# A hybrid DeltaNet and convolution layer: its 640 tokens go through the dense products as 128 and 512 columns in place of 320 and 320

## What is computed

```python
def _swiglu(h, w_in, w_out):
    a, b = jnp.split(h @ w_in, 2, axis=-1)
    return (jax.nn.silu(a) * b) @ w_out
...
    h = _rmsnorm(x, norm_ffn1) * (1 + sc1) + sh1
    x = x + 0.5 * gt1 * _swiglu(h, w_ffn1_in, w_ffn1_out)
    h = _rmsnorm(x, norm_mix) * (1 + sc2) + sh2
    m, s_f, s_b = _mixer(h, w_mix_in, ...)
    x = x + gt2 * m
    h = _rmsnorm(x, norm_ffn2) * (1 + sc3) + sh3
    x = x + 0.5 * gt3 * _swiglu(h, w_ffn2_in, w_ffn2_out)
```

## Time and profile before

| What | Value |
|---|---|
| Median of 2 runs | 1538.11 us (1537.68 to 1538.53) |
| Span of the profiled execution | 1540.2 us |
| TensorE matmuls, busy | 1444.7 us, 94% |
| TensorE weight loads, busy | 1395.0 us, 91% |
| VectorE, ScalarE, GpSimd busy | 41%, 25%, 10% |
| Matmul instructions | 9932 |

### The profile page before, as it was taken

The page is one execution under the profiler, slowest core; times in us unless marked ns, Lnnn a source line. Parts: engine busy times, 40 slices in busy tenths (PEclk is TensorE's granted clock), DMA queues, the critical chain, the costliest instruction groups (busy, mean ns, idle before and its releaser), DMA issues.

```text
span 1540.2 us, 23972 instructions
## 1 busy us (share of the span) xinstructions
PE 1444.7 (94%) x9932; PEld 1395.0 (91%) x9932; DVE 626.4 (41%) x995; ACT 385.1 (25%) x570; POOL 150.5 (10%) x113
## 2 busy tenths in 40 slices
PE   5699999999999969999997999987999999999996
PEld 3587899999999968999986999986999999999996
DVE  2722232333222255465585665446323332332222
ACT  3311211212111134453321212223222121212222
POOL 0300000000000030001334644003000000000000
PEclk9899999999999979999998999997999999999998
DMA  9488622222322211222545332121222222232211
GB/s 341 184 318 278 180 69 79 71 71 84 94 75 75 67 41 55 69 70 83 167 121 148 85 86 82 35 62 42 68 82 68 82 68 82 68 94 76 76 57 69
DMA packets 221201, 154.70 MB, mean 100 GB/s; under 512 B 22181, under 2 KB 207950, under 8 KB 217038
## 3 DMA queue, kind: packets, MB, share of 16 engines
q1 hardware_dynamic: 219680, 153.06, 32.4%
q10 hardware_dynamic: 1454, 0.68, 0.1%
HBM read 140.47 MB, written 13.24 MB: 100 GB/s over the span
## 4 chain that ended last, share of the span: by engine, by line
PE 87%; DVE 6%; ACT 2%; issue 2%; POOL 1%; DMA 1%; SPq 1%; ACTq 0%; DVEq 0%; POOLq 0%
PE ps L519 70%; PE ps L594 2%; PE ps L561 2%; PE ps L751 2%; PE ps L763 1%; PE ps L762 1%; DVE hf L1309 1%; DVE sub_tmp L1499 1%; PE ps L864 1%; PE ps L798 1%; DVE sub_x L1502 1%; POOL Tm L1790 1%; PE ps L800 1%; POOL NTa L1799 1%; PE ps L657 1%
## 5 line engine op out<-in xcount | busy, mean ns | idle before, releaser
L519 PE MATMUL ps<-h_hi,w_hi 128*128 128x320 f32 x1856 | 431.7, 314 | 9.6 <-DVE w_lo L1247 7.0
L519 PE MATMUL ps<-h_lo,w_hi 128*128 128x320 f32 x1856 | 424.7, 310 | 0.0
L519 PE MATMUL ps<-h_hi,w_lo 128*128 128x320 f32 x1856 | 424.3, 310 | 0.0
L1247 DVE TENSOR_TENSOR w_lo<-w_raw,w_hi 128x1024 fp32r<-128x1024 f32 (+1 forms) x156 | 207.8, 1333 | 430.7 <-ACT w_hi L919 429.4
L519 PEld LDWEIGHTS ps<-h_hi,w_hi 128*128 128x128 f32 x1856 | 311.6, 189 | 24.6 <-issue 18.8
L519 PEld LDWEIGHTS ps<-h_hi,w_lo 128*128 128x128 f32 x1856 | 312.1, 189 | 0.0
L519 PEld LDWEIGHTS ps<-h_lo,w_hi 128*128 128x128 f32 x1856 | 312.1, 189 | 0.0
L919 ACT ACTIVATE w_hi<-w_raw 128x1024 fp32r<-128x1024 f32 (+1 forms) x156 | 175.1, 1124 | 542.6 <-PE ps L519 474.8
L519 PE MATMUL ps<-g_hi,w_hi 128*128 128x320 f32 x704 | 160.9, 310 | 0.0
L519 PE MATMUL ps<-g_lo,w_hi 128*128 128x320 f32 x704 | 160.4, 309 | 0.0
L519 PE MATMUL ps<-g_hi,w_lo 128*128 128x320 f32 x704 | 160.3, 309 | 0.0
(11 more groups left out here) (221 smaller groups left out, 1271.2 us busy)
## 6 DMA issues: line engine op xcount, KB each, us to landing
w_raw<-in_w_ffn_in SPq DMA_DIRECT2D x88, 512.0 KB, 3.8
ada_w<-in_w_ada SPq DMA_DIRECT2D x32, 1024.0 KB, 6.9
w_raw<-in_w_ffn_out SPq DMA_DIRECT2D x32, 704.0 KB, 4.5
w_raw<-in_w_mix_in SPq DMA_DIRECT2D x28, 512.0 KB, 3.9
ada_w<-in_w_ada SPq DMA_DIRECT2D x8, 512.0 KB, 3.9
w_raw<-in_w_mix_out SPq DMA_DIRECT2D x8, 512.0 KB, 5.1
d_lt<-LTp SPq DMA_DIRECT2D x10, 256.0 KB, 2.4
d_qk<-QKp SPq DMA_DIRECT2D x10, 256.0 KB, 2.5
```

The lines of the kernel that those rows point to most:

```text
L519: last = pe.matmul(acc[a_slot][b], w, m[:, k0 + k, b * TH:b * TH + TH], start=start and k == 0 and n == 0, stop=stop and k == kt - 1 and n ...
L1247: nc.vector.tensor_tensor(w_lo[:, slot, 0:kt * P], w_raw[:, slot, 0:kt * P], w_hi[:, slot, 0:kt * P].bitcast(F32), ALU.subtract).then_inc( ...
```

## The change

The b loops take `PART[b]`, tokens 0 to 127 and 128 to 639, in place of two halves of 320. The first bank of an accumulator then holds the 128 context tokens and the second the 512 latent ones. The residual needs two instructions in place of three, the taps four in place of six. Everything else keeps its place and its count.

```diff
-TH = T // 2
+PART = (slice(0, TP), slice(TP, T))
...
-        acc = [[ps[2 * s][:, 0:TH], ps[2 * s + 1][:, 0:TH]] for s in (0, 1, 3)]
-        sums = [ps[4][:, 0:TH], ps[5][:, 0:TH]]
+        acc = [[ps[2 * s][:, 0:TP], ps[2 * s + 1][:, 0:TS]] for s in (0, 1, 3)]
+        sums = [ps[4][:, 0:TP], ps[5][:, 0:TS]]
...
-        PIECES = ((0, 0, TP, 0, 0), (0, TP, TH, 1, TP), (1, 0, TH, 1, TH))
...
                         for b in range(2):
-                            last = pe.matmul(acc[a_slot][b], w, m[:, k0 + k, b * TH:b * TH + TH],
+                            last = pe.matmul(acc[a_slot][b], w, m[:, k0 + k, PART[b]],
                                              start=start and k == 0 and n == 0,
                                              stop=stop and k == kt - 1 and n == 2)
...
                 for b in range(2):
-                    last = nc.scalar.activation(sa[:, b * TH:b * TH + TH], acc[0][b], ACT.Silu)
+                    last = nc.scalar.activation(sa[:, PART[b]], acc[0][b], ACT.Silu)
...
-                for bnk, b0, b1, i, t0 in PIECES:
+                for b in range(2):
                     last = nc.vector.scalar_tensor_tensor(
-                        out=x[:, j, t0:t0 + b1 - b0], in0=acc[a_slot][bnk][:, b0:b1], scalar=gate[:, m, j, i:i + 1],
-                        in1=x[:, j, t0:t0 + b1 - b0], op0=ALU.mult, op1=ALU.add)
+                        out=x[:, j, PART[b]], in0=acc[a_slot][b], scalar=gate[:, m, j, b:b + 1],
+                        in1=x[:, j, PART[b]], op0=ALU.mult, op1=ALU.add)
...
                 for step, (bnk, b0, b1, t0, tap) in enumerate((
-                        (0, 0, TP - 1, 1, before), (0, TP, TH, TP + 1, before), (1, 0, TH - 1, TH + 1, before),
-                        (0, 1, TP, 0, after), (0, TP + 1, TH, TP, after), (1, 0, TH, TH - 1, after))):
+                        (0, 0, TP - 1, 1, before), (1, 0, TS - 1, TP + 1, before),
+                        (0, 1, TP, 0, after), (1, 1, TS, TP, after))):
```

More of the change, by code:

```diff
@@ L593, in first_pair @@
                             for b in range(2):
-                                last = pe.matmul(acc[s][b], w, m[:, k, b * TH:b * TH + TH],
+                                last = pe.matmul(acc[s][b], w, m[:, k, PART[b]],
                                                  start=k == 0 and n == 0, stop=k == KD - 1 and n == 2)
@@ L690, in _ @@
                     for b in range(2):
-                        last = pe.matmul(sums[b], ones_t, (sa, uu)[n % 2][:, b * TH:b * TH + TH], start=True, stop=True)
+                        last = pe.matmul(sums[b], ones_t, (sa, uu)[n % 2][:, PART[b]], start=True, stop=True)
                     last.then_inc(ssm, 1)
@@ L698, in _ @@
                             for b in range(2):
-                                last = pe.matmul(sums[b][0:2 * NAB, :], wab_2[:, k, :, :], m[:, k, b * TH:b * TH + TH],
+                                last = pe.matmul(sums[b][0:2 * NAB, :], wab_2[:, k, :, :], m[:, k, PART[b]],
                                                  start=k == 0 and i == 0, stop=k == KD - 1 and i == 1)
@@ L1056, in _ @@
                     for b in range(2):
-                        last = nc.scalar.activation(abt[:, b * TH:b * TH + TH], sums[b][0:2 * NAB, :], ACT.Copy)
+                        last = nc.scalar.activation(abt[:, PART[b]], sums[b][0:2 * NAB, :], ACT.Copy)
                     last.then_inc(ab_ev, 1)
@@ L1091, in _ @@
                     for b in range(2):
-                        last = nc.scalar.activation(ss[:, n - 3, b * TH:b * TH + TH], sums[b], ACT.Copy)
+                        last = nc.scalar.activation(ss[:, n - 3, PART[b]], sums[b], ACT.Copy)
                     last.then_inc(ss_rdy, 1)
@@ L1103, in _ @@
                     for b in range(2):
-                        last = nc.scalar.activation(cv[:, b * TH:b * TH + TH], acc[2 if n == 2 else n % 2][b],
+                        last = nc.scalar.activation(cv[:, PART[b]], acc[2 if n == 2 else n % 2][b],
                                                     ACT.Identity, scale=tap)
@@ L1116, in _ @@
                     for b in range(2):
-                        last = nc.scalar.activation(zs[:, n - 12, b * TH:b * TH + TH], acc[n % 2][b], ACT.Silu)
+                        last = nc.scalar.activation(zs[:, n - 12, PART[b]], acc[n % 2][b], ACT.Silu)
                     last.then_inc(z_rdy, 1)
@@ L1125, in _ @@
                     for b in range(2):
-                        last = nc.scalar.activation(cc[:, b * TH:b * TH + TH], acc[n % 2][b], ACT.Copy)
+                        last = nc.scalar.activation(cc[:, PART[b]], acc[n % 2][b], ACT.Copy)
                     last.then_inc(cc_rdy, 1)
@@ L1333, in gate_out @@
                 for b in range(2):
-                    last = nc.vector.tensor_tensor(sa[:, b * TH:b * TH + TH], sa[:, b * TH:b * TH + TH], acc[1][b],
+                    last = nc.vector.tensor_tensor(sa[:, PART[b]], sa[:, PART[b]], acc[1][b],
                                                    ALU.mult)
@@ L1406, in taps @@
                 for step, (bnk, b0, b1, t0, tap) in enumerate((
-                        (0, 0, TP - 1, 1, before), (0, TP, TH, TP + 1, before), (1, 0, TH - 1, TH + 1, before),
-                        (0, 1, TP, 0, after), (0, TP + 1, TH, TP, after), (1, 0, TH, TH - 1, after))):
+                        (0, 0, TP - 1, 1, before), (1, 0, TS - 1, TP + 1, before),
+                        (0, 1, TP, 0, after), (1, 1, TS, TP, after))):
                     ins = nc.vector.scalar_tensor_tensor(out=cv[:, t0:t0 + b1 - b0], in0=a[bnk][:, b0:b1], scalar=tap,
                                                          in1=cv[:, t0:t0 + b1 - b0], op0=ALU.mult, op1=ALU.add)
-                    if step in (2, 5):
+                    if step in (1, 3):
                         link(ins)
@@ L1538, in _ @@
                     for b in range(2):
-                        last = nc.vector.tensor_tensor(uu[:, b * TH:b * TH + TH], cc[:, b * TH:b * TH + TH],
+                        last = nc.vector.tensor_tensor(uu[:, PART[b]], cc[:, PART[b]],
                                                        acc[a_slot][b], ALU.mult)
@@ L1559, in _ @@
                     for b in range(2):
-                        last = nc.vector.tensor_tensor(yc[:, m, b * TH:b * TH + TH], cv[:, b * TH:b * TH + TH],
+                        last = nc.vector.tensor_tensor(yc[:, m, PART[b]], cv[:, PART[b]],
                                                        acc[a_slot][b], ALU.mult)
```

## The result

The changed kernel takes 1718.24 us (median of 2 runs, 1717.95 to 1718.54) against 1538.11: 1.1167 of the time before, 95% interval 1.1146 to 1.1188. The forecast was 1711 us, in a range of 1680 to 1775.

The account below looks back on a forecast made before the run. TensorE's matmul pace was taken to bound the kernel: 4032 pairs going from 293.4 to 338 ns add 180 us, less 6 hidden and 1 saved, so 1538 + 173 = 1711 us, range 1680 to 1775.

Parts of the forecast that it names:

- the wide slot: Time from a 512-column fp32r matmul to the next matmul on TensorE, taken as 227 ns.
- The narrow slot: Time a 128-column matmul holds TensorE until the next matmul's weights are loaded, taken as 111 ns.
- only one load runs ahead: On TensorE, one weight load can run under the matmul before it, never two; read from rows behind line 657.
- rival 1: Two loads fit under a 512-column matmul, so the pair stays at 294 ns: 1537 us, chance 0.07.
- the low end: 128-column matmul at the bare weight load, 107 ns; with 15 us hidden 1687 us, range set from 1680.
- the tail of 162: Fixed 162 ns by which a matmul's recorded duration was taken to exceed its slot.
- the nearest row: Pricing the 512-column fp32r matmul, absent from the trace, by the bf16 one: 389 less 162 gives 227 ns.
- the upper end: 512-column matmul at 235 ns, if the 13.4 ns over its columns were a tenth of the stream.
- I let 7 us vanish: Taken off the 180 us: 6 us beside other work, 1 us for fewer residual and tap instructions.
- 4.7 (4 and 0.7): Mixing stage: 4 us hidden beside triangular solves and transfers, at most 0.7 us where units alternate with w_hi, w_lo and cv.
- The second: Narrow fp32r matmul falls to plain fp32's rate, 222 ns, pair 449 ns: 2156 us, chance 0.10.
- The third: Narrow matmul 124 ns or wide one 235, both 359 a pair: up to 1796 us; far end's chance 0.03.

Follow-up runs that it names:

- the two mirror-image runs: Changed kernel with 32 of 128 weight columns loaded in 3096 of 4032 pairs: for the 512-column matmul 1576.36 us, for the 128-column matmul 1723.84 us.

## Why the prediction was right

It was right in its sign, its mechanism and its size, 7 us under the first measurement and 11 under the second. But two terms of the sum were off by more than that, in opposite directions (over 4032 pairs the wide slot by 26 us, the narrow one by 17). That the size came out so near is in part luck.

**The narrow slot is the load.** Shown by the two mirror-image runs (1576 and 1724 us), by the line of the gate product, which kept its pace with 32 weight columns, and by the bend between 224 and 320 columns. The argument from the earlier trace rows that only one load runs ahead held too: with two, rival 1, the pair would have stayed at 294 ns.

**The durations of both slots were mis-sized, and their sum hardly.** I took 111 + 227 = 338. With the line from the runs a wide slot is 512 x 0.4516 + 2.2 = 233.4 ns, so 340.1 leaves 106.7 for the narrow one: the bare load of 128 x 0.833 that I had named as the low end. A second reading agrees. The wide matmuls of the run with 320 and 512 columns, where no load is bare, are recorded with this:

```profile
L520 PE MATMUL ps<-h_lo,w_hi 128*128 128x512 f32 x928 | 367.7, 396 | 0.0
```

Less the tail of 162 that is 234 ns. The changed kernel's are recorded with 443, 47 more, and 107 less the narrow stream's 60 (128 x 0.4516 + 2.2) is 47. The forecast that this group would last 389 ns on average failed for both reasons: the stream is longer than the bf16 row made it, and a matmul's record includes its wait for weights. The step that failed is "the nearest row": I let the bf16 matmul of 512 columns stand for fp32r, against the fp32r row of 320 columns scaled up (235), which I had as the upper end. The narrow slot's 111 came from plain fp32 matmuls of line 706, and the 4 ns over the load were not there. In the pair the errors were -6 and +4. The price of a load is not exact either: 106.7 fits 128 columns here, but the runs with 192 and 224 columns leave 109 and 110 ns for the narrow slot, and the load of 96 columns left 86 in place of 80.

**What is hidden.** I let 7 us vanish. 4032 x 46.7 ns are 188.3 us. The median grew by 180.1, so 8 us of them did not come; between the two kernels timed again (1722.33 against 1537.09) it grew by 185.2, so 3 did not; between the two profiled spans by 176.5, so 12 did not. The last figure is the least certain, because the profiled execution of the kernel before was a long one: its span alone is 2.1 us over the median of the times, where the changed kernel's is 1.5 under its own. So 7 is not shown to be wrong. The chain in order of time gives the places. The marks before and after:

```profile
621.82 42.24 PE ps L519 x288
816.59 0.89 SPq L337
949.37 0.39 issue
987.49 44.03 PE ps L519 x288
1031.54 1.15 DVE x L1376 x3
1068.14 336.19 PE ps L519 x2280
1523.81 1.15 DVE x L1376 x3
```

```profile
645.49 16.47 PE ps L593 x78
915.79 0.89 SPq L336
1046.66 0.40 issue
1086.54 49.24 PE ps L518 x288
1135.81 1.02 DVE x L1375 x2
1172.83 389.50 PE ps L518 x2280
1700.49 1.02 DVE x L1375 x2
```

| Stage, from mark to mark | Pairs | Due at 46.7 ns | Came |
|---|---|---|---|
| Inputs and first units, to 199.84 / 217.02 | 384 | 17.9 | 17.2 |
| The stretch of 2400 | 1200 | 56.0 | 56.0 |
| Residual, norm, first pair, to 585.21 / 661.96 | 48 | 2.2 | 3.6 |
| Mixer's strips, to 816.59 / 915.79 | 624 | 29.1 | 22.4 |
| Transfers and scan, to 949.37 / 1046.66 | 0 | 0 | -1.9 |
| Mixer's output, to 1031.54 / 1135.81 | 192 | 9.0 | 7.0 |
| Norm and first pair, to 1068.14 / 1172.83 | 48 | 2.2 | 0.4 |
| Second feed-forward, to 1523.81 / 1700.49 | 1536 | 71.7 | 72.0 |
| Output | 0 | 0 | -0.2 |

The strips hid 6.7 us, where I had 4.7 (4 and 0.7). In the two feed-forwards, where TensorE alone sets the pace, what was due came to within 0.3 us.

In three rows the clock has a part, and not only what is hidden. The mixer's output seems to hide 2 us. But in the trace of the kernel before the 288 matmuls there took 44.03 us, where 288 of the mixer's strips took 42.24. These are the windows of that stage, before and after, with the clock behind the five busy times:

```profile
985.00:1032.00 47.00, 44.68 (x293) 44.18 (x291) 21.52 (x37) 12.39 (x14) 0.00 (x0) 0.96 0.27 79
1084.00:1136.00 52.00, 50.21 (x294) 43.65 (x292) 20.57 (x29) 12.02 (x14) 0.00 (x0) 1.00 0.25 71
```

The kernel before had 0.96 of the clock there, the changed one 1.00. In the run with exchanged loops, which has the same pairs, the same 288 took 42.49 us. So most of the 2 us is the clock of these two executions. The same goes the other way for the first pair of the mixing stage, where 3.6 us came and 2.2 were due: its clock was 1.00 before (575 to 585) and 0.80 after (645 to 662), and 0.89 when the changed kernel was timed again. Before the second feed-forward the 66 matmuls took 10.80 us in the kernel before, at a clock of 0.93, and 9.96 with exchanged loops. The scan, in which the change moves nothing, got 1.9 us shorter. That repeats: between the same two marks it took 132.0 to 132.8 us in three traces with pairs of 293.4 ns (before, exchanged loops, 256 and 384), and 130.7 to 131.2 in three with 340.1 (after, timed again, residual in three). Its cause was not tried. Over a whole execution the clock was the same, as the prediction had it: 0.970 to 0.973 in the changed kernel timed again, 0.968 to 0.973 in the kernel before beside it.

**The rivals.** The second, fp32r at the rate of plain fp32, forecast 2156 us and is excluded: the narrow matmuls stream in 60 ns when the load lets them. The third had the narrow slot at 124 ns or the wide one at 235: the narrow one was 106.7, the wide one 233.4, near the second.

## What to carry to other kernels

In this kernel a matmul hid its successor's weight load only where its stream was longer than that load; here the load takes 107 ns for 128 weight columns and by the same numbers the bend should lie near 230 fp32r columns (an estimate; the runs show it between 224 and 256, as 256 and 384 cost nothing), so split a free size so that no part is under it, and 256 and 384 is as good as 320 and 320. Where a narrow part can't be avoided, what counts is the weight load of the matmul behind it, not its own. A price for an operation that the trace lacks is better scaled from the same data type at another size than from another type at the same size.

## What the runs showed that I had not expected

- fp32r streams 640, 832 and 960 columns a pair in 293.4, 380.1 and 437.9 ns at the full granted clock: 0.4516 ns a column and 2.2 ns a matmul, 8% over a column per cycle at 2.4 GHz. The order of the banks does not matter to it. The cause of the 8% is open.
- A matmul's recorded duration includes its wait for weights: 443 ns behind a bare load, 395 or 396 without, for the same 512 columns.
- Near the bend the terms don't add exactly: pairs with 192 and 224 columns took 2 to 3 ns more than load and wide stream (106.7 + 204.5 = 311.2 against 313.4, and 340.1 against 343.4), and a 32-column stream 3.6 ns more than a 128-column one.
